# Second-block attention: a tile's transposes issued two slots behind its scores, with three buffers of exponentials

## The reference, cut to what matters

```
# even layer, latent queries: 8 heads, 512 queries, 768 keys; then the context's own 256 queries x 256 keys
s = jnp.einsum('bhgqd,bhkd->bhgqk', qblk, k_all).astype(jnp.float32) * A_SCALE
p = jax.nn.softmax(s, axis=-1).astype(v_all.dtype)
return jnp.einsum('bhgqk,bhkd->bhgqd', p, v_all)

# odd layer: per query row, keys of 8 rows x 16 columns near it, with a bias, and 256 context keys
s_loc = jnp.einsum('bhqd,bhiqjd->bhqij', qr, kw).astype(jnp.float32) * C_SCALE + bias.astype(jnp.float32)
s_ctx = jnp.einsum('bhqd,bhkd->bhqk', qr, kc_h).astype(jnp.float32) * C_SCALE
p = jax.nn.softmax(jnp.concatenate([s_loc..., s_ctx], axis=-1), axis=-1).astype(vw.dtype)
```

## Time and profile before

| | before |
|---|---|
| runs, median (lowest to highest) | 4791.59 us (4785.71 to 4803.49) |
| the profiled execution, its own time | 4773.82 us |
| its span, first to last instruction | 4772.0 us |
| mean granted TensorE clock over the span | 0.876 of 2.4 GHz |
| PE busy, share of the span | 3626.6 us, 76% |
| DVE busy | 2743.4 us, 57% |
| ACT busy | 1930.8 us, 40% |
| "ae" phase | about 2277 to 2436 us |
| "ao" phase | about 3590 to 3852 us |

### The profile page before, as it was taken

How to read it: one execution, slowest core, us unless ns; L and a number is a source line. 1 busy time by engine, 2 the same in 40 slices (tenths; PEclk the granted TensorE clock), 3 DMA queues, 4 the chain that set the end, 5 groups by cost and what they waited for, 6 DMA issues and landing times. The chain is left out here.

```text
span 4772.0 us, 46449 instructions
## 1 busy us (share of the span) xinstructions
PE 3626.6 (76%) x16838; PEld 2839.8 (60%) x16838; DVE 2743.4 (57%) x3131; ACT 1930.8 (40%) x2166; POOL 174.3 (4%) x236
## 2 busy tenths in 40 slices
PE   7487776759888858964884798885697865888882
PEld 5287564647777743152663677774575655777771
DVE  3743437438888841135533788886415645888882
ACT  2211123226666631020431666663313423666660
POOL 0032000000000000000000000001001100000000
PEclk9699897869999978986895999998797877999996
DMA  3700120249999945721013899996310035999983
GB/s 95 267 1 1 58 74 1 71 159 353 361 359 358 358 140 190 250 75 51 1 45 120 321 355 361 362 359 228 99 36 17 11 107 196 364 358 357 355 322 128
DMA packets 254815, 921.43 MB, mean 193 GB/s; under 512 B 54484, under 2 KB 77396, under 8 KB 180948
## 3 DMA queue, kind: packets, MB, share of 16 engines
q1 hardware_dynamic: 232652, 839.45, 48.8%
q10 hardware_dynamic: 13968, 50.86, 2.6%
q0 software_dynamic: 8064, 29.36, 1.7%
HBM read 820.54 MB, written 99.06 MB: 193 GB/s over the span
## 5 line engine op out<-in xcount | busy, mean ns | idle before, releaser
L170 DVE TENSOR_TENSOR f3e_w_lo<-f_raw,f3e_w_hi 128x2048 fp32r<-128x2048 f32 x192 | 439.2, 2289 | 99.4 <-ACT f3e_w_hi L165 99.2
L170 DVE TENSOR_TENSOR f1e_w_lo<-f_raw,f1e_w_hi 128x2048 fp32r<-128x2048 f32 x192 | 439.2, 2289 | 99.0 <-ACT f1e_w_hi L165 98.8
L170 DVE TENSOR_TENSOR f2e_w_lo<-f_raw,f2e_w_hi 128x2048 fp32r<-128x2048 f32 x192 | 439.2, 2289 | 98.1 <-ACT f2e_w_hi L165 98.0
L165 ACT ACTIVATE f3e_w_hi<-f_raw 128x2048 fp32r<-128x2048 f32 x192 | 366.4, 1911 | 30.3 <-issue 18.6
L165 ACT ACTIVATE f1e_w_hi<-f_raw 128x2048 fp32r<-128x2048 f32 x192 | 366.5, 1911 | 27.8 <-issue 16.1
L165 ACT ACTIVATE f2e_w_hi<-f_raw 128x2048 fp32r<-128x2048 f32 x192 | 366.4, 1911 | 27.7 <-issue 16.0
L2083 PE MATMUL ada_psum_acc<-ada_w,ada_sT 128*2 128x512 f32 x384 | 167.3, 599 | 13.6 <-DMA ada_w<-in_ada_w_dram 13.6
L176 PE MATMUL f3e_psum_gate<-f3e_w_hi,f3e_xT_hi 128*128 128x512 f32 x256 | 110.4, 431 | 72.2 <-issue 70.5
L176 PE MATMUL f1e_psum_gate<-f1e_w_hi,f1e_xT_hi 128*128 128x512 f32 x256 | 111.4, 435 | 70.0 <-issue 69.3
L176 PE MATMUL f2e_psum_gate<-f2e_w_hi,f2e_xT_hi 128*128 128x512 f32 x256 | 109.5, 428 | 72.2 <-issue 70.7
L176 PE MATMUL l_psum_acc<-l_w_hi,m_hT_hi 128*128 128x512 f32 x288 | 116.5, 404 | 41.8 <-DVE l_w_lo L170 41.8
(11 more groups left out here) (781 smaller groups left out, 9771.6 us busy)
## 6 DMA issues: line engine op xcount, KB each, us to landing
f_raw<-in_moe_w_dram SPq DMA_DIRECT2D x384, 1024.0 KB, 7.3
f_raw<-in_w_gate_dram SPq DMA_DIRECT2D x64, 1024.0 KB, 6.9
f_raw<-in_w_up_dram SPq DMA_DIRECT2D x64, 1024.0 KB, 6.8
f_raw<-in_w_down_dram SPq DMA_DIRECT2D x64, 1024.0 KB, 8.0
ada_w<-in_ada_w_dram SPq DMA_DIRECT2D x24, 2048.0 KB, 8.1
xbuf<-m_zeros SPq DMA_DIRECT2D x11, 2048.0 KB, 18.9
f1e_xin<-xbuf SPq DMA_DIRECT2D x33, 512.0 KB, 7.1
f2e_xin<-xbuf SPq DMA_DIRECT2D x33, 512.0 KB, 7.3
```

The source lines that it names most:

```text
L165: return act.activation(dst, src, ACT.Copy)
L170: return v.tensor_tensor(dst, src, hi.bitcast(F32), ALU.subtract)
```

## The change

```diff
-    PV0 = 3
+    TURN = 2
+    PROBS = TURN + 1
+    PV0 = TURN + 2
     PVN = 3
     B_SLOT = PV0 + PVN - 1
...
-        if 1 <= j <= nj:
-            order += [("p", n) for n in range(first_piece[j - 1], first_piece[j])]
+        if TURN <= j < nj + TURN:
+            order += [("p", n) for n in range(first_piece[j - TURN], first_piece[j - TURN + 1])]
...
-        pr = prob or [s.sb(f"prob{i}", [P, width])[:, :] for i in range(2)]
+        pr = prob or [s.sb(f"prob{i}", [P, width])[:, :] for i in range(PROBS)]
...
-                        mm = pe.transpose(... cols(pr[j % 2]) ...)
+                        mm = pe.transpose(... cols(pr[j % PROBS]) ...)
...
-                if 1 <= j <= nj:
-                    turn(j - 1)
+                if TURN <= j < nj + TURN:
+                    turn(j - TURN)
...
-                    if j >= 2:
-                        act.wait_ge(t_done, first_piece[j - 1])
-                    act.activation(pr[j % 2][:, 0:l["n"]], ...
+                    if j >= PROBS:
+                        act.wait_ge(t_done, first_piece[j - PROBS + 1])
+                    act.activation(pr[j % PROBS][:, 0:l["n"]], ...
...
-                if 1 <= j <= nj:
-                    i, g = j - 1, jobs[j - 1]["g"]
+                if TURN <= j < nj + TURN:
+                    i, g = j - TURN, jobs[j - TURN]["g"]
...
-                if 2 <= j <= nj + 1:
-                    i, g = j - 2, jobs[j - 2]["g"]
+                if TURN + 1 <= j <= nj + TURN:
+                    i, g = j - TURN - 1, jobs[j - TURN - 1]["g"]
...
-            attend_phase(nc, "ae", ..., prob=[pj[:, i, 0:NTA * P] for i in range(2)],
+            attend_phase(nc, "ae", ..., prob=[pj[:, i, 0:NTA * P] for i in (0, 1, 4)],
...
-                         prob=[ctx[:, i, 0:640] for i in range(2)],
+                         prob=[ctx[:, i, 0:640] for i in range(2)]
+                         + [w.sb("prob", [P, 640])[:, :]],
```

More of the change, by code:

```diff
@@ L791, in turn @@
                     for k, cols in enumerate(piece["cols"]):
-                        mm = pe.transpose(bank[:, k * P:(k + 1) * P], cols(pr[j % 2]), tab[:, C_IDENT:C_IDENT + P])
+                        mm = pe.transpose(bank[:, k * P:(k + 1) * P], cols(pr[j % PROBS]), tab[:, C_IDENT:C_IDENT + P])
                     mm.then_inc(t_done, 1)
@@ L849, in _ @@
                     act.wait_ge(max_done, j + 1)
-                    if j >= 2:
-                        act.wait_ge(t_done, first_piece[j - 1])
-                    act.activation(pr[j % 2][:, 0:l["n"]], psS[:, l["s0"]:l["s0"] + l["n"]], ACT.Exp,
+                    if j >= PROBS:
+                        act.wait_ge(t_done, first_piece[j - PROBS + 1])
+                    act.activation(pr[j % PROBS][:, 0:l["n"]], psS[:, l["s0"]:l["s0"] + l["n"]], ACT.Exp,
                                    bias=nm[:, j:j + 1], accum_out=sm[:, j:j + 1]).then_inc(exp_done, 1)
-                if 1 <= j <= nj:
-                    i, g = j - 1, jobs[j - 1]["g"]
+                if TURN <= j < nj + TURN:
+                    i, g = j - TURN, jobs[j - TURN]["g"]
                     if g >= 2 and i % GJ == 0:
@@ L2529, in even_mixer @@
                          scale=1.0, dst=turned(kT), **common)], NTA * P)
-            attend_phase(nc, "ae", tab, even_groups(qT, kT, vp, oT), prob=[pj[:, i, 0:NTA * P] for i in range(2)],
+            attend_phase(nc, "ae", tab, even_groups(qT, kT, vp, oT), prob=[pj[:, i, 0:NTA * P] for i in (0, 1, 4)],
                          row=[pj[:, i, 0:512] for i in (2, 3)])
```

## The result

| | before | after |
|---|---|---|
| median (lowest to highest), runs | 4785.3 us (4771.8 to 4803.5), 20 | 4808.5 us (4793.1 to 4828.5), 20 |
| ratio, 95% interval | | 1.0049 (1.0038 to 1.0060) |
| profiled execution, its own time | 4773.8 us | 4804.1 us |
| first scores of "ae" to its last normalization | 156.5 us | 170.5 us |
| the same of "ao" | 259.7 us | 271.9 us |

The change made the kernel 23 us slower, where +5 was forecast: at 4808.5 us it lies inside the range of 4777 to 4818, and the 23 us are on the very edge of "within 0.5%" (24 us). The base of the forecast was the median of three runs, 4791.6 us; the 20 runs of the kernel before have 4785.3 us. The phase marks are read from the timelines.

A forecast was written before the change was run, and what follows sets the result against it. PE's queue was taken to set the pace, idling mostly for DVE to empty PSUM places. The terms -0.4 + 5.4 - 2.2 + 1.0 + 1.1 = +4.9 us on 4791.6 gave 4796.5 us, range 4777 to 4818.

The forecast's parts named there:

- The wait for the exponentials and the ring: PE's waits in both phases: for exponentials -0.4 us; for a place among three PSUM banks, 0 of 43.5 us removed.
- rival 1: The third buffer fills PE's idle ahead of transposes: up to 43.5 us faster, 4748 us; chance 0.07.
- C slots: In "ao", C scores 640 columns instead of 512: 0.36 us longer in each of 15 slots, +5.4 us.
- Rival 4: In "ao", a longer C lets DVE catch up in D, so the pairing costs nothing: 4791 us; chance 0.18.
- A slots of "ao": They score 512 columns instead of 640: 0.16 to 0.38 us shorter each, 8 x 0.27 = -2.2 us.
- Starts: The third tile's scores now precede the first transposes: 1.90 us more in "ao", 2.22 us in "ae".
- The ends: One more slot runs without scores at each phase's end: 0.92 us back in "ao", 1.1 us in "ae".
- the sum for "ae": Exponentials' wait -0.4 us, start and end net +1.1 us; "ae" should last 159 + 1 us.
- the point at which the forecast is wrong altogether: Sign set for failure: either phase moves by over 15 us, or the rest of the kernel moves.
- Rival 2: The clock falls a slot earlier in "ao", ahead of D's scores: 26 us above the forecast, 4823 us; chance 0.15.
- Rival 3: The clock stays up longer in A and C slots of "ao": -16 us, with the sum -11, 4781 us; chance 0.10.
- the mark set for rival 2: Sign in the profile after: a clock of "ao" under 0.77, where the forecast said 0.80 to 0.82.

The follow-up runs named there:

- before_lofirst: Kernel before, with DVE making the low parts ahead of the add and the maximum in each slot: 4776.7 us, 0.9994 (0.9975 to 1.0012).
- after_fill: Changed kernel, with each D slot's first piece transposed three times in "ae", six in "ao", filling PE's wait: 4779.4 us, 0.9998 of the kernel before.
- before_late: Kernel before, with the scores of tile 0 of "ae" made twice, so the rest of "ae" comes later: 4791.1 us, 1.0017 (1.0003 to 1.0030).
- the second looks: Changed kernel, and the kernel with the change in "ae" alone, each profiled again unedited: "ae" 170.4 and 179.4 us.

## Why the prediction was right, and where it was wrong

The time lies in the range, but not for the reasons forecast: the change costs 23.2 us and not 4.9, and by the estimate above most of that is the clock. The base was 6.3 us too high, which hid a third of the miss, and the rest fell into the room that the range leaves above the forecast of 4790 to 4803. That part is luck.

*The wait for the exponentials and the ring: right.* Ring waits 8.4 and 35.8 us against 10.1 and 33.4; rival 1 (the third buffer fills the bubbles) is out, and before_lofirst shows the releaser to be DVE's order: change that order and the wait goes; add a buffer and it stays. Of the two readings of the Trainium skill's rule on consistent bubbles (Perfetto Trace Analysis, Identifying Performance Opportunities), the trace after agrees with the one for PSUM: an SBUF buffer more took nothing off the 43.5 us. No PSUM was added in any run; an earlier release alone took the ring's wait from 33.4 to 4.1 us.

*C slots: right.* +0.36 us was said, 2.99 became 3.36 and 3.46 became 3.83; the wait of 0.55 us was in the band of 0.5 to 0.6 (0.43 in the C slots with a spread). There are 14 such slots and not 15, so the term should have been +5.0; measured is +5.9, with some low clock in it. Rival 4 (nothing for the pairing) is out.

*A slots of "ao": right in size where the clock was alike* (4.73 to 4.55, -0.18 in the band of 0.16 to 0.38), but that was so in four of the seven odd ones; in the other three A took 5.4 to 5.5 us, against 4.7 before. The sum is +0.2 and not -2.2 us.

*Starts: right* (+1.9 and +2.2 us, said 1.90 and 2.22). The ends gave back 2.2 us in "ao", where 0.92 was said, and 1.6 in "ae", where 1.1 was said.

*"ae": wrong.* The step that failed is the sum for "ae", "-0.4" and "+1.1": it priced the clock in "ae" at nothing. In its place the runs show 37.4 us more of low-clock time (36.3 to 73.7), 32 of them in the seven A slots, which grew by 12.1 us. The phase moved by 14 us, near the 15 that I had named as the point at which the forecast is wrong altogether. I looked for a fall of the clock only where the change lengthens an idle, in "ao". In "ae" no idle grew: D's is 1.06 us before and after (0.94 in every second group). It was already followed by partly low A slots (5.96, 5.07, 5.01 us), which I hadn't read, and after the change by low ones without exception.

*Rival 2: the mechanism was right, its place wrong.* It had the clock fall ahead of D's scores in "ao". Every second D slot kept 3.36 us, and in the others the fall came up to 1.1 us before their end, behind their scores; the low clock lasted longer, into the B slots (+5.8 us), and "ae" paid the larger part. Rival 3 (the clock stays up) is out with it. The clock of "ao" was 0.77, under the 0.80 to 0.82 of the forecast and at the mark set for rival 2, from another slot. The Trainium skill's description of kernels whose clock swings because of short idles between groups of matmuls (TensorE: Matmul & The Clock Gate, A second HAM failure mode: psum-queue depth-cycling) agrees with after_fill, where filling such an idle of 1.06 us takes the swing away from the A slots of "ae".

*What stays open.* Why the same idle of 1.06 us is followed by a low A slot every time at a distance of two slots and only sometimes at one. A later start alone is excluded by before_late, chance by the second looks. That the clock's rise falls another 1 us into the first A slot, and the rest follows from that, is a reading that fits all profiles of unfilled kernels with DVE's old order here and that no run tests. Open too is why the 256-key slots of "ae" run at half clock in some programs and not in others.

## What to carry to other kernels

More distance between two stages helps only if the wait is for the earlier stage; read the releaser, and if it is the emptying of a place, look first at the order of the engine that empties it. After such a cut, read which wait comes next before you count the gain: here 29 us of one wait turned into 20 us of two others and a slower clock. And an idle of a microsecond that comes back with every group is to be priced with the clock of the slot behind it, by reading every such slot and not one.

## What the runs showed of the hardware

- The same stretch of PE work, with no idle in it, took 3.49 us at a granted clock of 1.00 and 6.35 us at 0.50, behind the same idle of 1.06 us. Slots that no edit touched lost as much: the 256-key slots of "ae" took 1.66 us in one kernel and 2.94 us in another.
- In one execution, seven A slots behind D slots with at most 0.3 us of idle ran at a clock of 1.00 (3.42 us, before_lofirst), and the seven behind an idle of 1.49 us at 0.50.
- Redundant transposes in a wait of 1.06 us left the D slot at 3.33 us, and with those of "ao" won back 24 us in the changed kernel. Where the clock was low anyway they made the first D slot 0.84 us longer (5.39 for 4.55). In the kernel before the gain isn't clear of none (0.9989, 0.9973 to 1.0004).
- A kernel's scatter from run to run (before spread over 32 us in 20 runs) goes with its low-clock time, at 0.30 us for each us, with a correlation of 0.95.
